# Rotated heads go through device memory, loads and gathers are placed by step, items are spread evenly

## The reference

```python
h = jnp.einsum('bnd,de->bne', x, w_in)
qa, ka, va, ga, qb, kb, vb, gb = jnp.split(h, IN_SPLITS, axis=-1)
qa = _rope(qa...); ka = _rope(ka...)
out_a = _dilated_attention(qa, ka, va) * jax.nn.silu(ga)
qb = _axial_rope(_rms_norm_heads(qb, q_norm), row, col)
kb = _axial_rope(_rms_norm_heads(kb, k_norm), row, col)
out_b = _gqa_attention(qb, kb, vb) * jax.nn.silu(gb)
f = jnp.einsum('bne,ed->bnd', jnp.concatenate([out_a, out_b], -1), w_out)
return _layer_norm(DEEPNORM_ALPHA * x + f, ln_g, ln_b)
```

## Time and profile before

| what | value |
|---|---|
| median of 3 runs | 513.11 us (510.29 to 513.71) |
| profiled execution, its own time | 511.76 us |
| its span | 510.0 us |
| mean granted TensorE clock | 0.936 |
| busy: PE, DVE, ACT, POOL | 428.6, 256.7, 219.9, 226.9 us |
| bytes moved on SyncE's queue | 44.09 MB |
| first scores of the loop | 60.52 us |

### The profile page before, as it was taken

The page is one execution under the profiler, slowest core; times in us unless marked ns, Lnnn a source line. Parts: engine busy times, 40 slices in busy tenths (PEclk is TensorE's granted clock), DMA queues, the critical chain, the costliest instruction groups (busy, mean ns, idle before and its releaser), DMA issues.

```text
span 510.0 us, 7179 instructions
## 1 busy us (share of the span) xinstructions
PE 428.6 (84%) x2566; PEld 378.6 (74%) x2566; DVE 256.7 (50%) x606; ACT 219.9 (43%) x466; POOL 226.9 (44%) x247
## 2 busy tenths in 40 slices
PE   5999880999896778998789999967988798699991
PEld 4889860899695568788678899856877586578880
DVE  3516400453577525666466446346565666525564
ACT  5421301464336425554555335333565866421222
POOL 4547301443647611532942454235432882344574
PEclk9999996799899979999899999979799899899997
DMA  8640566220200450200062203641330412122123
GB/s 307 229 126 22 132 154 168 64 62 22 63 21 22 108 124 17 63 21 22 1 190 60 62 22 92 155 126 41 82 105 22 164 58 110 44 102 63 41 90 117
DMA packets 21188, 44.56 MB, mean 87 GB/s; under 512 B 3872, under 2 KB 3872, under 8 KB 21152
## 3 DMA queue, kind: packets, MB, share of 16 engines
q1 hardware_dynamic: 21152, 44.09, 29.6%
HBM read 27.56 MB, written 3.15 MB: 60 GB/s over the span
## 4 chain that ended last, share of the span: by engine, by line
PE 58%; SPq 11%; DVE 10%; POOL 6%; ACT 6%; issue 5%; DMA 3%; ACTq 0%; DVEq 0%
PE acc L540 8%; PE acc L541 8%; PE acc L542 8%; SPq L390 8%; PE o_ps L606 6%; PE pt_ps L472 4%; SPq L382 3%; PE s_ps L482 2%; PE acc L630 2%; PE acc L631 2%; PE acc L632 2%; PE pt_ps L482 2%; POOL rot L1078 2%; POOL rot L1077 2%; DVE prob L943 2%
## 5 line engine op out<-in xcount | busy, mean ns | idle before, releaser
L1065 POOL TENSOR_TENSOR w_lo<-raw,w_hi 128x512 fp32r<-128x512 f32 x55 | 72.9, 1334 | 135.2 <-ACT w_hi L670 135.1
L1114 POOL TENSOR_SCALAR prob<-prob,den 128x512 f32<-128x512 f32 (+1 forms) x96 | 60.7, 637 | 95.5 <-DVE den L958 95.5
L540 PE MATMUL acc<-t_hi,w_lo 128*128 128x512 f32 (+1 forms) x256 | 91.6, 358 | 0.0
L732 ACT ACTIVATE prob<-prob,nmax 128x512 f32<-128x512 f32 (+1 forms) x96 | 62.2, 648 | 67.6 <-DVE nmax L943 67.6
L541 PE MATMUL acc<-t_lo,w_hi 128*128 128x512 f32 (+1 forms) x256 | 88.9, 347 | 0.0
L542 PE MATMUL acc<-t_hi,w_hi 128*128 128x512 f32 (+1 forms) x256 | 88.6, 346 | 0.0
L606 PE MATMUL o_ps<-p_hi,v_st 128*128 128x256 f32 x160 | 47.6, 313 | 25.6 <-DVE mix_t L967 14.4
L951 DVE TENSOR_TENSOR p_lo<-pt_ps,p_hi 128x512 fp32r<-128x512 f32 x80 | 54.7, 685 | 19.2 <-ACT p_hi L740 19.2
L740 ACT ACTIVATE p_hi<-pt_ps 128x512 fp32r<-128x512 f32 x80 | 47.4, 593 | 29.7 <-PE pt_ps L472 27.1
L670 ACT ACTIVATE w_hi<-raw 128x512 fp32r<-128x512 f32 x55 | 33.4, 622 | 60.9 <-DMA raw<-w_in 45.5
L472 PE MATMUL pt_ps<-cst,prob 128*128 128x128 f32 x320 | 51.6, 288 | 9.5 <-POOL prob L1114 9.5
(11 more groups left out here) (204 smaller groups left out, 867.7 us busy)
## 6 DMA issues: line engine op xcount, KB each, us to landing
raw<-w_in SPq DMA_DIRECT2D x48, 256.0 KB, 2.7
ka_st<-rot SPq DMA_DIRECT2D x64, 96.0 KB, 2.1
q_st<-rot SPq DMA_DIRECT2D x48, 96.0 KB, 2.2
raw<-w_out SPq DMA_DIRECT2D x16, 256.0 KB, 2.8
mix_t<-xt SPq DMA_DIRECT2D x8, 384.0 KB, 6.2
tab<-consts SPq DMA_DIRECT2D x3, 512.0 KB, 5.1
q_st<-mix_t SPq DMA_DIRECT2D x16, 96.0 KB, 2.2
rot<-x_prompt SPq DMA_DIRECT2D x3, 512.0 KB, 6.6
```

What stands on the lines that cost most here:

```text
L540: nc.tensor.matmul(out, a_lo, b_hi, start=(k == 0), stop=False)
L732: ins = nc.scalar.activation(s, s, ACT.Exp, scale=-1.0, bias=nmax[:, j % 2, t:t + 1], accum_out=den[:, j % 2, t:t + 1])
L1065: nc.gpsimd.tensor_tensor(w_slot(g)[1], raw_slot(g), w_slot(g)[0].bitcast(F32), ALU.subtract) \
L1114: ins = nc.gpsimd.tensor_scalar(s, s, den[:, j % 2, t:t + 1], 0.5, ALU.mult, ALU.mult)
```

## The change

**Staging.** Each rotated chunk has a tensor in device memory, `between`, of shape (2 parts, 4 heads, 2 halves, 32, 768). SyncE writes a chunk into it with four transfers (part x half) of 128 partitions x 768, 384 KB each, whose pattern on the device side is (4, 32, 768) with a step of 64 rows between heads (`spill`). It waits until they have landed (`spilled`), and reads head by head: a query with one transfer of 384 KB whose source pattern is (2, 64, 768), a head's keys with two transfers whose source pattern is (2, 64, 768) with step 0 in the first dimension. The next chunk may overwrite `rot` when the one before has been written out, no longer when every head has been gathered.

**SyncE** follows the steps: `load_step` says at which step a slice is issued, `staged_at` when a head is read. **Sums of squares** run two steps after their item, ahead of the step's projection on PE, and count on a semaphore of their own (`ssq_read`). GpSimd's rotation of QB0 and QB1 waits for the products only, and its `query_power` comes a step later. **PACE** spreads the items of steps 16 to 54 evenly: the steps of the last items of QB0, QB1, KA1, QA1, GA1 were 14, 33, 46, 54, 63 and are 14, 28, 41, 53, 65. The rotated chunks are written out three steps after those (17, 31, 44, 56).

The diff, cut to its core:

```diff
-PACE = ((0, 0), (15, 9), (16, 11), (34, 17), (43, 20), (55, 29), (64, 32))
+PACE = ((0, 0), (15, 9), (16, 11), (54, 29), (66, 32))
...
+        between = {c: nc.dram_tensor(f"between{n}", (2, 4, 2, HALF, TOK), F32, kind="Internal").ap()
+                   for n, c in enumerate(("k", "q", C_QB0, C_QB1, C_KA1, C_QA1))}
...
+        def staged_at(u):
+            at = {(c, i): max(step_of[(c, 2)] + 3, 0 if c == C_KA1 else UNITS * (FIRST_HEAD[c] + i - 3) + 1)
+                  for c in rot_chunks for i in range(4)}
+            return [k for k in at if at[k] == u]
+        def before_in_rot(c):
+            return "k" if c == C_QB0 else rot_chunks[rot_chunks.index(c) - 1]
...
+        def load_step(g):
+            c = chunk_of_slice(g) if g < IN_SLICES else len(CHUNKS)
+            first = g - FIRST_SLICE[c]
+            if first >= 4:
+                return {4: step_of[(C_GA1, 1)], 5: step_of[(C_GA1, 2)]}.get(first, 59 + first)
+            item = [(c - 2, 1), (c - 2, 2), (c - 1, 0), (c - 1, 0)][first]
+            return step_of.get(item, 0)
+        def loads_at(u):
+            return [g for g in range(FIRST_SLICE[C_VKB], IN_SLICES + 10) if load_step(g) == u]
...
+            def spill(c):
+                low, high = rotation_buffers(c)
+                for part, src in enumerate((high, low)):
+                    for e in range(2):
+                        sp.dma_start(between[c][part, :, e], src[:, e]).then_inc(spilled[c], 16)
             def stage_query(j, c):
-                low, high = rotation_buffers(c)
-                rows = slice(32 * (j % 4), 32 * (j % 4) + 32)
                 if j >= 4:
                     sp.wait_ge(s_ready, UNITS * (j - 3))
-                for n, src in enumerate((high[rows, 0], high[rows, 1], low[rows, 0], low[rows, 1])):
-                    sp.dma_start(q_st[32 * n:32 * n + 32, j % 4, :].bitcast(F32), src).then_inc(q_staged[j % 4], 16)
-
-            def stage_keys(slot):
-
-                low, high = rotation_buffers("k")
-                rows = slice(32 * slot, 32 * slot + 32)
-                for part, src in enumerate((high, low)):
-                    for n in range(4):
-                        sp.dma_start(ka_st[32 * n:32 * n + 32, part, slot, :].bitcast(F32), src[rows, n % 2]) \
-                            .then_inc(ka_staged[slot], 16)
+                src = between[c][:, j % 4].rearrange("s e p t -> s (e p) t")
+                sp.dma_start(q_st[:, j % 4, :].bitcast(F32), src).then_inc(q_staged[j % 4], 16)
+            def stage_keys(slot, c):
+                if c != "k":
+                    sp.wait_ge(s_ready, UNITS * (slot + 1))
+                for part in range(2):
+                    src = between[c][part, slot].rearrange("e p t -> (e p) t")
+                    sp.dma_start(ka_st[:, part, slot, :].bitcast(F32), src[None].to_broadcast([2, HEAD_DIM, TOK])) \
+                        .then_inc(ka_staged[slot], 16)
...
             load_chunk(C_GA0)
             sp.wait_ge(rot_lo, 1)
-            stage_keys(0)
+            spill("k")
             sp.wait_ge(rot_lo, 2)
+            spill("q")
+            sp.wait_ge(spilled["k"], 64)
+            stage_keys(0, "k")
+            sp.wait_ge(spilled["q"], 64)
             stage_query(0, "q")
-            for j in range(1, 4):
-                stage_keys(j)
-                stage_query(j, "q")
-            sp.dma_start(tab[:], consts[:, C_TAB + 2 * SEQ:C_TAB + 4 * SEQ].rearrange("p (a b) -> p a b", a=2)) \
-                .then_inc(tab_loaded, 16)
-            for c in range(C_VKB, C_QB1 + 1):
-                load_chunk(c)
-            for kv in range(N_KV_B):
-                sp.wait_ge(acc_read, index[(KEYS_T, 1)] + 1)
-                for part in range(2):
-                    here, there = ((0, HEAD_DIM), (HEAD_DIM, 0))[kv]
-                    sp.dma_start(kb_st[there:there + HEAD_DIM, part, kv, :].bitcast(F32),
-                                 kb_st[here:here + HEAD_DIM, part, kv, :].bitcast(F32)) \
-                        .then_inc(kb_staged, 16)
-            sp.wait_ge(rot_lo, rot_count(C_QB0))
-            for j in range(4, 8):
-                stage_query(j, C_QB0)
-            load_chunk(C_GB1)
-            load_chunk(C_KA1)
-            sp.wait_ge(rot_lo, rot_count(C_QB1))
-            sp.dma_start(tab[:], consts[:, C_TAB:C_TAB + 2 * SEQ].rearrange("p (a b) -> p a b", a=2)) \
-                .then_inc(tab_loaded, 16)
-            for j in range(8, 12):
-                stage_query(j, C_QB1)
-            load_chunk(C_VA1)
-            load_chunk(C_QA1)
-            sp.wait_ge(rot_lo, rot_count(C_KA1))
-            for slot in range(4):
-                stage_keys(slot)
-            load_chunk(C_GA1)
-            for i in range(2):
-                load_slice(IN_SLICES + i)
-            sp.wait_ge(rot_lo, rot_count(C_QA1))
-            for j in range(12, 16):
-                stage_query(j, C_QA1)
-            for i in range(2, 8):
-                load_slice(IN_SLICES + i)
+            for u in range(STEPS):
+                for g in loads_at(u):
+                    load_slice(g)
+                if u < 3:
+                    stage_keys(u + 1, "k")
+                    stage_query(u + 1, "q")
+                if u == 3:
+                    load_tables(2)
+                if u == step_of[(KEYS_T, 1)] + 1:
+                    for kv in range(N_KV_B):
+                        double_keys(kv)
+                for c in rotations_at(u - 3):
+                    sp.wait_ge(rot_lo, rot_count(c))
+                    if c == C_QB1:
+                        load_tables(0)
+                    spill(c)
+                    sp.wait_ge(spilled[c], 64)
+                for c, i in staged_at(u):
+                    if c == C_KA1:
+                        stage_keys(i, c)
+                    else:
+                        stage_query(FIRST_HEAD[c] + i, c)
             for j in range(4):
-                sp.wait_ge(q_staged[j], 16 * 4 * 4)
+                sp.wait_ge(q_staged[j], 64)
...
+                for item in squares_at(u - 2):
+                    square_sums(item)
                 for item in items_at(u):
                     project(item)
-                for item in squares_at(u - 1):
-                    square_sums(item)
...
-                    if n == 0 and c == C_QB0:
+                    if n == 0:
                         dve.wait_ge(tab_loaded, 32)
-                        for slot in range(4):
-                            dve.wait_ge(ka_staged[slot], 128)
-                    elif n == 0:
-                        for slot in range(4):
-                            dve.wait_ge(q_staged[slot], 64 * 2)
+                        dve.wait_ge(spilled[before_in_rot(c)], 64)
...
+                elif kind(c) == QUERY_B:
+                    pool.wait_ge(products_done, square_items.index((c, 2)) + 1)
                 else:
-                    pool.wait_ge(acc_read, index[(c, 2)] + 1)
+                    pool.wait_ge(*read(index[(c, 2)]))
...
-                for c in rotations_at(u - 2):
+                for c in rotations_at(u - 3):
```

More of the change, by code:

```diff
@@ L248, in ready, with read @@
             return i + 3
+        def read(i):
+            squares = len([item for item in items[:i + 1] if kind(item[0]) == QUERY_B])
+            if i < N_IN and kind(items[i][0]) == QUERY_B:
+                return ssq_read, squares
+            return acc_read, i + 1 - squares
         def in_bank(i):
@@ L393, in _, with double_keys @@
+            def double_keys(kv):
+                sp.wait_ge(*read(index[(KEYS_T, 1)]))
+                here, there = ((0, HEAD_DIM), (HEAD_DIM, 0))[kv]
+                for part in range(2):
+                    sp.dma_start(kb_st[there:there + HEAD_DIM, part, kv, :].bitcast(F32),
+                                 kb_st[here:here + HEAD_DIM, part, kv, :].bitcast(F32)).then_inc(kb_staged, 16)
             for k in range(KT):
@@ L452, in _ @@
                 sp.dma_start(res(t), x_rows(t)).then_inc(x_back[t], 16)
-            for i in range(8, 10):
-                load_slice(IN_SLICES + i)
             sp.wait_ge(pt_ready, NU)
@@ L511, in bank_free @@
                 if i >= 3:
[L512 removed]
+                    pe.wait_ge(*read(i - 3))
             def project(item):
@@ L872, in evacuate @@
                         dve.wait_ge(tab_loaded, 48)
-                        for slot in range(4):
-                            if c == C_KA1:
-                                dve.wait_ge(q_staged[slot], 64 * 3)
-                            else:
-                                dve.wait_ge(ka_staged[slot], 256)
+                        dve.wait_ge(spilled[before_in_rot(c)], 64)
                     dve.wait_ge(acc_ready, ready(i))
```

26 lines of the change are left out of this document (16 added, 10 removed).

## The result

| what | before | after |
|---|---|---|
| median of 4 runs each | 513.41 us (510.29 to 514.25) | 714.29 us (710.98 to 715.20) |
| profiled span | 510.0 us | 708.8 us |
| mean granted TensorE clock | 0.936 | 0.819 |

The ratio of after to before is 1.392, with a 95% interval of 1.384 to 1.399: the change costs 201 us.

The account below looks back on a forecast made before the run. TensorE was taken to set the time, idling behind new transfers on 4 or 2 DMA engines. Span 510.0 plus 170.8 gave 680.8; lower clock after five stops made 690.8, time outside the span 692.6; forecast 692 us, range 620 to 765.

Parts of the forecast that it names:

- The chain: Stops followed from first scores at 111 us to step 62 at 548.4, which is 170.8 us later than before.
- rotated 2 later: At QB1, KA1 and QA1: the chunk is rotated 2 us later, before its write and closing of 18.8 us.
- SyncE's issue time costs nothing: On SyncE: 56 new issues replace 128 of some 0.63 us, and the DMA engines' queue is the fuller one.
- Rival A: New transfers are dealt over all 16 DMA engines, so the small terms decide: 484 us; chance 0.13.
- (a): Early copies shrink to 8 writes and 12 reads between loads; the 16.3 us stop goes: net 11 us gained.
- (b): Head 4's query, which waits 6.34 us at 181.11, would be there some 4 us earlier.
- (c): Sums of squares a step later take away most of PE's short waits for sq: 2 us.
- (d): Items spread over the steps remove idle, with the lower clock and the small o_ps waits: 8.5 us.
- (f): Last gate item two steps later leaves output slice 5 one step instead of three after slice 3: 4 us charged.
- (e): Second half's 32 key copies go, with the 4.93 us stop at 341.01 and its lower clock: 6.3 us.
- B: Transfers use 16 engines but each round trip is late, before heads 0, 4, 12 and output slice 5: 506 us; chance 0.03.
- C: Reads use few engines but weight loads pass them, so slices no longer stop ACT: 610 us; chance 0.04.

Follow-up runs that it names:

- experiments 1 to 4: Changed kernel with new transfers on 16 engines, 481.41 us; only reads so, 555.34; only writes so, 651.19; kernel before plus lone transfers of each count, 82 us more.
- experiment 4: Kernel before, with 384 KB transfers of outermost counts 16, 8, 4, 2 alone, then three count-2 reads and a slice, after its last store: 82 us more than before.
- e1_all16: The changed kernel, same round trips, with every new transfer cut or laid out to outermost counts of 128 or 32, so all 16 engines: 481.41 us.
- experiment 6: Kernel before, with VKB's first slices issued ahead of the copies of heads 1 to 3: 494.58 us, 0.963 of before.
- experiment 7: e1_all16 with the first chunk's keys and queries copied directly from SBUF to SBUF, without the round trip: 472.21 us, 0.921 of before.
- experiment 9: e1_all16 with the sums of squares one step after their item and behind the projection, as before: 487.73 us, 0.950 of before.
- experiment 8: e1_all16 with the item placement (PACE) of the kernel before: 506.11 us, 0.988 of before.

## Why the prediction held, step by step

**What was forecast.** 692 us, by transfers on 4 and 2 engines in one line; measured 714.29, 3% more and inside the range. The profiled execution took 710.98, of which 2.2 lie outside the span. The mechanism is shown: by the window shares, by the packets and by experiments 1 to 4. That the number came so near is in part luck: terms put some 35 us too low and some 13 us too high (below) stand against each other.

**Prices.** A read was put at 7.9 us and a chunk's writes at 16.8. Four writes took 16.00 us to issue behind four others, and from the first issue of a chunk's writes to its first read are 20.2 to 20.8 us (416.49 to 436.71 for KA1), where write and closing were put at 18.8. Per engine 25 to 26 GB/s against 23.4 to 24.9. Two readings behind the range were slightly off: the best slice in the earlier trace rows is 428, not 422, and at 21.8 GB/s the 322 us become 361, not 358. That moves its ends by 4 us at most. The page gives no time to landing for the few-engine transfers; alone they took 7.3 to 10.3 us (experiment 4), at the edge of the forecast "10 us or more".

**The chain.** First scores 111, measured 110.65. Step 9 at 190.5, measured 192.52, with the cause that was named: ACT, and DVE behind it, wait for a slice that is queued behind heads 1 to 3. Head 4's query 265.2, measured 273.66. Step 22 at 285.3, measured 283.84, but not as it was reckoned: some 12 us of stop were put ahead of it, and PE stopped 4.04 us inside it. The slices of step 37 were put at 366.9; that stop ends at 383.99. The stop behind KA1's eight reads 480.2, measured 505.92 (it caught the transposes of step 52, not ACT's slice for step 49 alone). Step 62 at 548.4, measured 570.61.

**The term that was mis-sized** is "rotated 2 later", with the "write 18.8" behind it. By 2 us after a step's start the chunk's last item was to be rotated, that is, ready for SyncE to write out. Measured, and by how much it is later than put, in us:

| chunk (step) | start of the step, start of the writes | later than put | writes to first read, beyond 18.8 |
|---|---|---|---|
| QB0 (17) | writes at 242.74, put at 237.5 | 5.2, of it 2.0 inherited from step 9 | 1.9 |
| QB1 (31) | 334.72 to 341.01 | 4.3 | 1.5 |
| KA1 (44) | 409.82 to 416.49 | 4.7 | 1.4 |
| QA1 (56) | 521.32 to 529.06 | 5.7 | 2.0 |

Four pieces on three engines must follow each other: for QB0 DVE's products end at 232.3, GpSimd's sums at 236.0, ACT's rounding at 237.9, and DVE's low part runs from 241.0 to 242.7. The rotations come to 17.9 us, the writes to 6.8, and with the 2.0 from step 9 that makes 26.7. Step 62 is only 22.2 late, because the rest adds up to some 4.5 us the other way: the stop behind KA1's reads caught PE in step 52, three steps further than put, so that 15.4 us were left to step 56 and not 21.2 (5.8 less); from QA1's first read to step 62 passed 20.7 and not 26.2 (5.5 less); the stop near step 37 ended 22.7 us after QB1's first read and not 18.3 (4.4 more); KA1's reads with what follows them took 69.2 and not 65.7 (3.5 more); and the remainder is 1.2 less.

**The clock.** Ten us were charged for five stops. From step 62 to the end the profiled run needed 708.8 − 570.6 = 138.2, where 132.4 and those 10 were put; the charge belonged in the steps behind each stop rather than at the end. Against the kernel with all engines, all stops together cost 13.2 us of longer busy time.

**"SyncE's issue time costs nothing"** was right for the time and wrong in its picture. Single issues took up to 8 us, where issues into a queue with transfers on 16 engines took 0.6; the first scores came at 110.65 without any term for it.

**Rival A's sum was near, its parts were not.** It gave 484 for transfers on 16 engines; e1_all16 is such a kernel and takes 481.41. Part by part:
- (a) 11: early copies 18.9 (experiment 6) less the round trip 9.2 (experiment 7) are 9.7.
- (b) 4: head 4's stop shrinks from 6.34 to 3.87 us, 2.5.
- (c) 2: measured 6.3 (experiment 9).
- (d) with (f) 4.5: measured 24.7 (experiment 8), within which is the 4.93 us stop.
- (e) 6.3: not measured by itself. In e1_all16 the key transfers are 32 again, so the gain from their going was not there to be had, and the stop vanished all the same, by the spacing of (d). The cause that (e) names, slices behind key transfers, is in the traces of experiment 8; the spacing decides whether PE feels it.

The measured parts exceed the 32 us in all, so they are not additive: with the old PACE head 12 waits 5.17 us for its round trip, with the new one 1.3. How far each interaction goes was not measured.

**Rivals B and C.** B's round trips cost 9.2 us for the first chunk and 5.9 more for heads 4 and 12 (472.21 to 466.36), 15 where it had put 22, and the rest of the change outweighs them. C is refuted by experiment 4 and by ACT's waits.

## What to carry to other kernels

Before a transfer's pattern is changed, read the outermost count of both of its sides: with 4 or 2 there, 384 KB took 4.0 and 7 to 8 us in a row, where four small copies of 96 KB took 4 x 0.63 = 2.5 us to issue. A scratch tensor laid out in another order, with the reads cut to 32 rows, turned 714 us into 481. When PE waits for DVE or GpSimd while the DMA row shows 1 or 2 tenths, follow the wait to the load that stands behind a slow transfer. And a stop can hang on two conditions at once. The late slice behind the key transfers and the dense items both stood at the 4.93 us stop; the experiment that spread the items removed it and says nothing on what removing the transfers would do. A cause is ruled out only by a run in which that cause is gone.

## What was not expected of the hardware

- An issue on SyncE is held while the queue is full of transfers on few engines: 5.8 us for the third read of count 2, 7.35 for a 16-engine slice behind it, 16.00 for four writes of count 4, against some 0.5 for an issue into an empty queue.
- A lone write of count 4 takes 8.5 us and a lone read 7.3, while four such writes behind four others were issued in 16.00, or 4.0 each; about 6 was expected for either alone. At count 16 it is 3.4 and 3.8. Windows of the probe, over the writes of count 16, 4 and 2:

```profile
513.00:516.00 3.00, 0.00 (x0) 0.00 (x0) 0.00 (x0) 0.00 (x0) 0.00 (x0) 0.50 0.50 131
530.50:538.50 8.00, 0.00 (x0) 0.00 (x0) 0.00 (x0) 0.00 (x0) 0.00 (x0) 0.50 0.19 49
546.50:556.00 9.50, 0.00 (x0) 0.00 (x0) 0.00 (x0) 0.00 (x0) 0.00 (x0) 0.50 0.12 41
```

Four engines work three quarters of the 8 us of their write (0.19 x 16 / 4), two nearly all of the 9.5 us of theirs (0.12 x 16 / 2 = 0.96). Why four are slower alone than in a row was not found out.
